# Attention rows exponentiated and scaled two groups ahead of their turns, and two copies of projected tiles moved ahead of squares and rows

## The chip, the cores and the metric

The kernel runs on one core of a Trainium2 chip. The metric is the device time of one execution in microseconds (us), the median of several executions; lower is better. The engines are TensorE (PE; its weight loads are listed as PEld), VectorE (DVE), ScalarE (ACT), GpSimd (POOL) and SyncE (SP), which only issues DMAs here.

## The reference

One inference step of a two-layer trunk over 1072 tokens: 1024 frames of a new stream, 16 meta tokens before it, and 32 frames of a running stream with 128 cached ones. Per layer, cut to what matters:

```python
h = rms_norm(x, gains[0])
z = h @ w_in          # q, k, v, indexer q/k/weights, conv B/C/x, gates
score = jnp.einsum('bqh,bqhl->bql', wi, jax.nn.relu(s))     # indexer
_, idx = lax.top_k(score, topk)                             # keys per query
p = jax.nn.softmax(jnp.where(valid, logits, -jnp.inf), axis=-1)
o = jnp.einsum('bqhgk,bqkhd->bqhgd', p, vg)                 # 8 heads over 2 key heads
m = jax.nn.sigmoid(ga) * y_a + jax.nn.sigmoid(gb) * y_b
x = x + rms_norm(m @ w_o, gains[1])
f = jnp.square(jax.nn.relu(rms_norm(x, gains[2]) @ w_up)) @ w_down
x = x + rms_norm(f, gains[3])
```

All of it is in float32; outputs are the new activations and the new keys, values, indexer keys and convolution states.

## The kernel before, in words

Activations are kept transposed: features on the 128 partitions, 8 feature tiles (`KT`), tokens along the free axis in three thirds of 358 columns (`side(i)`, `NCH`). Every matrix product is done in three passes of high and low parts: `H[:, 0]` is the rounded high part, made by ACT (`h_rows`, L1053), `H[:, 1]` the remainder, made by DVE (`lo` in `hn_rows`, L1561). Each engine runs a list of instructions written out by hand, in order; semaphores tie the lists together, so an instruction that waits holds back all that stand behind it on its engine.

**Projection.** `proj(n)` (L643, matmuls L660) multiplies token tile `ORDER[n]` (the 48 special tokens first, then tiles 0 to 7 of 128 tokens) by the 1092 columns of q, k, v and the indexer, into PSUM banks 0 to 2: 8 steps k of 9 matmuls. `proj(n + 1)` reuses the banks and so waits for `sb_copied`, which ACT's `copy_out(n)` (L1123) signals when it has copied the banks to `SB`. `put_v(n)` (L1137) then copies the values to `V`. `proj(1)` also waits until both parts of all eight H rows of the second third in time are there (`hq_hi`, `hq_lo`). While this runs, the norm of the last third is still being made: ACT squares the eight feature tiles (`edge_squares`, L1049), DVE adds them (in layer 0 L1532 and L1535), PE sums over partitions (`edge_sums`, L626) and broadcasts (L634), DVE scales (L1565), and ACT and DVE make the H rows of that third. DVE's `rotate` (L1638) applies the rotary embedding to `SB`, ACT's `stage` stores keys and values and makes `ST`, which PE transposes (L674); ACT copies the transposes to `IQ`, `IK` and `QH`. The indexer's scores (PE L692, ACT L1120, DVE L1684 and L1687) follow tile by tile.

**Search, convolution, gates.** DVE then finds the top-k thresholds by a bitwise search (L1836 and around), while PE does the convolution and gate products (L558) from weights that POOL splits (L440, L442).

**Attention.** The work is cut into 18 groups i = 2a + kv: query tile `ORDER[a]` (48 special tokens, then tiles 0 to 7) by key head kv, four query heads each. A group has as many *turns* as it has key tiles: 2 for a = 0 and 1, then 3, 4, ... 9. `STEPS` lists all turns in order. The stages of a row (group i, head g) are

- `logits(i, g)` on PE (L821), into one of two pairs of PSUM banks, so that a row waits for the masking of the row before last;
- `mask_row(i, g)` on DVE (L1900, and L1889 for the meta columns of the longest tile, g = -1): adds the mask, scales, and takes the least value;
- `exponent(i, g)` on ACT (L1284): exponential, with its sum;
- `normalise(i, g)` on DVE: reciprocal (L1909) and scaling (L1911).

A turn is `turn_p(u)` on PE (four transposes, L838), the copy to `PT` on ACT, and `values(u)` on PE (L850). After the last turn of a group DVE copies the result (`outputs`, L1921), ACT makes its high part (`o_hi_copy`) and DVE its remainder (`o_lo_part`, L1928).

The order on each engine before, for group i: PE does `logits(i + 2, g)` in turn min(g, n - 1), then the transposes of the next turn, then `values`. ACT, behind the PT copy of turn min(g, n - 1):

```python
copy(PT[0:w, u % 3, 0:GROUP * m], PS[0:w, 4 + u % 2, 0:GROUP * m]).then_inc(pt_made, 1)
for g in range(GROUP):
    if now + 1 < NGRP and min(g, n - 1) == kt:
        exponent(now + 1, g)
```

DVE, per group: `mask_row(i + 2, g)` and `normalise(i + 1, g)` in turn, with `outputs(i - 1)` behind the first mask row and `o_lo_part(i - 2)` behind the third. So a row is masked two groups ahead, and exponentiated and scaled one group ahead, and its last rows are scaled just before the group's first turn. The rows live in three sets of buffers (`prob`): groups i, i + 1 and i + 2 have one each.

## Time and profile before

| | |
|---|---|
| runs shown | 3441.95, 3443.53, 3445.90 us; median 3443.53 |
| profiled execution | 3440.69 us, its span 3438.9 us |
| busy over the span | PE 96%, PEld 91%, DVE 55%, ACT 22%, POOL 33% |
| chain that ended last | PE 88%, DVE 6%, ACT 2%, the rest 1 to 2% each |
| attention stages | about 557 to 751 us and 2256 to 2451 us |
| projection stages | begin of the span to about 220 us, and from about 1730 us |

The span is that of the profiled execution alone; its own time with what lies around it is in the table. In a timeline a row gives the start, the duration, the engine, the line, the operation with output and input, how often it follows itself, and in brackets how long the engine had been idle before it and what released it. In a table of windows the granted clock is a mean over the window between the two levels of TensorE, 1.00 being 2.4 GHz and 0.50 being 1.2 GHz.

### The profile page before, as it was taken

The page shows a single profiled execution, that of the slowest core. Times are in us where ns is not written, and L with a number is a line of the kernel's source. Part 1 is how long each engine was busy: PE and PEld are TensorE (multiplying, and loading weights), DVE is VectorE, ACT ScalarE, POOL GpSimd, SP SyncE. Part 2 cuts the span into 40 slices and gives each one's busy share as a digit, 9 for nine tenths or more (in the row PEclk, how much of TensorE's full clock was granted, in tenths as well). Part 3 has the DMA queues.
Part 4 walks back from the last instruction along what each step waited for, and adds up shares of the span by engine and source line. Part 5 has one row for each costly group of instructions (what it writes and reads, how often), then busy time and mean ns, then how long its engine had stood idle before and what let it go on. Part 6 is the DMA issues. An engine that isn't in the chain of part 4 may idle for free.

```text
span 3438.9 us, 48630 instructions
## 1 busy us (share of the span) xinstructions
PE 3288.3 (96%) x19268; PEld 3120.4 (91%) x19268; DVE 1883.4 (55%) x3093; ACT 770.1 (22%) x1370; POOL 1125.3 (33%) x517
## 2 busy tenths in 40 slices
PE   4999998999999999999969999989999999999997
PEld 4989997679999999999959999966799999999997
DVE  6259997644662332415562799966456614233245
ACT  4330113641320110101233201136314201011011
POOL 2023332005444333434420333310163434334460
PEclk8999998999999999999989999989999999999999
DMA  3121223013221111111331112220133111111113
GB/s 127 51 68 44 75 93 107 25 45 110 97 83 43 49 43 43 43 49 43 105 99 57 68 44 81 94 94 19 69 114 105 60 43 43 49 43 43 43 61 103
DMA packets 97867, 230.02 MB, mean 67 GB/s; under 512 B 13024, under 2 KB 54592, under 8 KB 97728
## 3 DMA queue, kind: packets, MB, share of 16 engines
q1 hardware_dynamic: 36448, 126.50, 11.3%
q10 hardware_dynamic: 61280, 101.61, 8.5%
q8 instruction: 94, 1.54, 0.2%
q14 instruction: 45, 0.37, 0.0%
HBM read 176.44 MB, written 51.65 MB: 66 GB/s over the span
## 4 chain that ended last, share of the span: by engine, by line
PE 88%; DVE 6%; ACT 2%; issue 2%; DMA 1%; POOL 1%; ACTq 1%; DVEq 0%; SPq 0%; POOLq 0%
PE PS L558 61%; PE PS L567 9%; PE PS L660 5%; PE PS L850 5%; PE PS L821 2%; PE PS L838 2%; PE PS L730 1%; PE PS L692 1%; PE PS L674 1%; DVE HN L1565 1%; DVE X L1610 1%; DVE H L1561 1%; DMA HN<-in_xT 1%; DVE X L1616 1%; ACT SB L1024 1%
## 5 line engine op out<-in xcount | busy, mean ns | idle before, releaser
L558 PE MATMUL PS<-H,W 128*128 128x358 f32 x8064 | 1329.8, 327 | 0.1
L558 PEld LDWEIGHTS PS<-H,W 128*128 128x128 f32 x8064 | 1327.6, 189 | 0.2
L440 POOL TENSOR_TENSOR W<-RAW,ones 128x1024 fp32r<-128x1024 f32 x184 | 358.7, 1949 | 1667.5 <-PE PS L558 1626.2
L558 PE MATMUL PS<-A,W 128*128 128x358 f32 x4608 | 760.1, 327 | 0.0
L558 PEld LDWEIGHTS PS<-A,W 128*128 128x128 f32 x4608 | 758.7, 189 | 1.5 <-issue 1.5
L442 POOL TENSOR_TENSOR W<-RAW,W 128x1024 fp32r<-128x1024 f32 x184 | 511.7, 2781 | 14.4
L1836 DVE TENSOR_SCALAR_CACHE_REDUCE PASS<-SC,TC,CST 128x400 bf16<-128x400 f32 x372 | 356.1, 1020 | 1.7
L660 PE MATMUL PS<-WQ,H 128*128 128x364 f32 (+1 forms) x1296 | 245.4, 346 | 46.2 <-ACT SB L1024 38.6
L660 PEld LDWEIGHTS PS<-WQ,H 128*128 128x128 f32 (+1 forms) x1296 | 219.1, 190 | 58.6 <-ACT SB L1024 41.5
L2000 DVE TENSOR_TENSOR SQ<-SQ,RS 128x1074 f32<-128x1074 f32 x64 | 117.8, 1841 | 263.6 <-ACT SQ L1410 257.8
L1410 ACT ACTIVATE SQ<-PS 128x1074 f32<-128x1074 f32 x64 | 68.4, 1069 | 808.9 <-PE PS L558 806.6
L2015 DVE TENSOR_TENSOR X<-X,PS 128x1074 f32 x32 | 40.8, 1274 | 306.6 <-PE PS L558 306.6
L2002 DVE TENSOR_TENSOR SQ<-SQ 128x1074 f32<-128x1074 f32 x64 | 205.8, 3216 | 2.2
L850 PE MATMUL PS<-PT,V 128*128 128x512 f32 (+3 forms) x368 | 202.5, 634 | 0.3
L567 PE MATMUL PS<-A,WD 128*128 128x358 f32 x1008 | 168.0, 327 | 0.0
L567 PE MATMUL PS<-H,WR 128*128 128x358 f32 x1008 | 168.0, 326 | 0.0
L567 PEld LDWEIGHTS PS<-A,WD 128*128 128x128 f32 x1008 | 165.1, 188 | 0.0
L567 PEld LDWEIGHTS PS<-H,WR 128*128 128x128 f32 x1008 | 164.5, 188 | 0.0
L821 PEld LDWEIGHTS PS<-KS,QS 128*128 128x128 f32 (+1 forms) x480 | 87.3, 206 | 79.2 <-issue 60.7
L821 PE MATMUL PS<-KS,QS 128*128 128x512 f32 (+6 forms) x480 | 145.0, 425 | 6.1 <-DMA QS<-qs_keep 3.4
L1024 ACT ACTIVATE A<-SQ 128x1074 f32 (+1 forms) x64 | 70.6, 1103 | 341.7 <-DVE SQ L2002 341.7
L1024 ACT ACTIVATE PT<-PS 128x512 f32<-128x512 f32 (+3 forms) x184 | 107.4, 584 | 159.4 <-PE PS L838 159.2
(182 smaller groups left out, 2938.3 us busy)
## 6 DMA issues: line engine op xcount, KB each, us to landing
RAW<-in_w_slab SPq DMA_DIRECT2D x216, 512.0 KB, 3.5
gates<-GS ACTq DMA_DIRECT2D x32, 537.0 KB, 3.0
x_keep<-X ACTq DMA_DIRECT2D x9, 1432.0 KB, 7.3
GA<-gates ACTq DMA_DIRECT2D x16, 537.0 KB, 3.6
GB<-gates ACTq DMA_DIRECT2D x16, 537.0 KB, 4.5
ALO<-x_keep ACTq DMA_DIRECT2D x6, 1432.0 KB, 7.3
qs_keep<-QH ACTq DMA_DIRECT2D x16, 512.0 KB, 2.6
QS<-qs_keep ACTq DMA_DIRECT2D x16, 512.0 KB, 3.6
```

The lines of the kernel that those rows point to most:

```text
L440: g_.tensor_tensor(hi, raw, one, ALU.mult).then_inc(hi_split, 1)
L442: g_.tensor_tensor(lo, raw, hi.bitcast(F32), ALU.subtract).then_inc(raw_split, 1)
L558: mm = nc.tensor.matmul(PS[:, b0 + c, 0:CW], W[:, s, w, k, :], act[:, a, k, c * CW:(c + 1) * CW], start=(first and w == 0 and a == 0), sto ...
L567: mm = nc.tensor.matmul(PS[:, bank_, 0:CW], w[:, h, k, :], act[:, a, k, c * CW:(c + 1) * CW], start=(k == first and h == 0 and a == 0), st ...
L660: last = nc.tensor.matmul(PS[0:m, b, 0:QG], H[:, a, k, t * P:t * P + m], WQ[:, k, w, b * QG:(b + 1) * QG], start=(k == 0 and w == 0 and a ...
L821: last = nc.tensor.matmul(flat[0:m, c0 + dst:c0 + dst + w], QS[:, a % 3, GROUP * kv + q, 0:m], KS[:, 2 * kv + x, key:key + w], start=(x == ...
L838: last = nc.tensor.transpose(PS[0:w, 4 + u % 2, g * m:(g + 1) * m], prob(PA, i, g)[0:m, dst:dst + w], cst["ident"][0:m, 0:m])
L850: nc.tensor.matmul(PS[:, 6 + kv, 0:GROUP * m], V[0:w, vt, :], PT[0:w, u % 3, 0:GROUP * m], start=(kt == 0), stop=(kt == len(key_tiles(t)) ...
L1024: return nc.scalar.activation(out, in_, ACT.Copy)
L1836: did(V_.tensor_scalar(PASS[0:m, SC_OFF[t]:SC_OFF[t] + EXT[t]], row(t), at_least, cst["negk"][0:m, c:c + 1], op, ALU.add, accum_out=CNT[0: ...
L2000: V_.tensor_tensor(SQ[:, s, :], SQ[:, s, :], RS[:, :], ALU.mult).then_inc(up_scaled, 1)
L2002: V_.tensor_tensor(SQ[:, s, :], SQ[:, s, :], SQ[:, s, :], ALU.mult).then_inc(up_sq, 1)
```

## The change

1. *Attention.* `rows_at(u)` lists the rows whose logits PE does in turn u; PE's own order is what it was. ACT now does the exponentials of those rows behind the PT copy of turn u + 1, and DVE scales them in turn u + 1, both for group i + 2. DVE's start order mixes the mask rows of group 1 with the scaling of group 0, and `outputs` and `o_lo_part` are placed by turn.
2. *Projection.* In layer 0 the copy of tile 0 and of its values stand after six of the eight H rows of the second third, ahead of the last two, of `past_split` and of the squares of the last third; in layer 1 they stand after two of those squares. In both layers the copy of tile 1 stands after four of the last third's H rows. No instruction is added or taken away.

```diff
--- before.py
+++ after.py
@@ -378,6 +378,13 @@
         STEPS = [(a, kv, kt) for a in range(9) for kv in range(NKV) for kt in range(len(key_tiles(ORDER[a])))]
         NU = len(STEPS)
 
+        def rows_at(u):
+
+            a, kv, kt = STEPS[u]
+            n = len(key_tiles(ORDER[a]))
+            return [(j, g) for j, g in ROW_UNITS if j == NKV * a + kv + 2 and min(max(g, 0), n - 1) == kt]
+
+
         ENDS = [u + 1 for u, (_, _, kt) in enumerate(STEPS) if u + 1 == NU or STEPS[u + 1][2] == 0]
 
         def raw_q(l, k):
@@ -856,11 +863,9 @@
                     if i < 2:
                         logits(i, g)
                 turn_p(0)
-                for u, (a, kv, kt) in enumerate(STEPS):
-                    i, n = NKV * a + kv, len(key_tiles(ORDER[a]))
-                    for j, g in ROW_UNITS:
-                        if j == i + 2 and min(max(g, 0), n - 1) == kt:
-                            logits(j, g)
+                for u in range(NU):
+                    for j, g in rows_at(u):
+                        logits(j, g)
                     if u + 1 < NU:
                         turn_p(u + 1)
                     values(u)
@@ -1100,9 +1105,7 @@
             wq_high(0, range(5, 6))
             edge_root(0, 0, 1)
             wq_high(0, range(6, 8))
-            h_rows(0, 1, range(KT))
-            past_split(0)
-            edge_squares(0, 2, range(KT))
+            h_rows(0, 1, range(6))
 
             for l in range(DEPTH):
 
@@ -1165,26 +1168,36 @@
                     wq_high(l, range(6, 7))
                     h_rows(l, 1, range(4, KT))
                     wq_high(l, range(7, 8))
-                    edge_squares(l, 2, range(KT))
+                    edge_squares(l, 2, range(2))
+                    copy_out(0)
+                    put_v(0)
+                    edge_squares(l, 2, range(2, KT))
                 def cc_copy(j):
                     act.wait_ge(slab_done, l * NDONE + S_CONV + 3 * j + 1)
                     if j:
                         act.wait_ge(conv_drained, l * 8 + 2 * j - 1)
                     copy(ch(CC[:, :]), bank(conv_bank(3 * j))).then_inc(cc_drained, 1)
 
-                copy_out(0)
+                if l == 0:
+                    copy_out(0)
+                    put_v(0)
+                    h_rows(0, 1, range(6, KT))
+                    past_split(0)
+                    edge_squares(0, 2, range(KT))
                 act.wait_ge(past_lo, (l + 1) * 2)
                 act.dma_start(d["ks_keep"][:, :, PAST0:NKEY], KH[:, :, :].bitcast(F32)).then_inc(past_stored, 16)
-                put_v(0)
                 edge_root(l, 0, 2)
                 stage(0)
-                h_rows(l, 2, range(KT))
+                h_rows(l, 2, range(4))
+                copy_out(1)
+                h_rows(l, 2, range(4, KT))
                 act.wait_ge(hq_lo, (l + 1) * NCH * KT)
                 if l:
                     act.wait_ge(edge_stored, l * NCH * 16)
                 for n, t in enumerate(ORDER):
                     m, nn = ROWS[t], l * 9 + n
-                    copy_out(n + 1)
+                    if n:
+                        copy_out(n + 1)
 
                     act.wait_ge(turned, l * 27 + 3 * n + 1)
                     if n:
@@ -1286,19 +1299,20 @@
 
                 for g in range(GROUP):
                     exponent(0, g)
+                behind = [(1, g) for g in range(GROUP)]
                 i = 0
                 for u, (a, kv, kt) in enumerate(STEPS):
-                    t, now = ORDER[a], NKV * a + kv
-                    m, w, n = ROWS[t], key_tiles(t)[kt][2], len(key_tiles(t))
+                    t = ORDER[a]
+                    m, w = ROWS[t], key_tiles(t)[kt][2]
                     if kv == 0 and kt == 0 and 0 < a < 7:
                         q_load(a + 2)
                     act.wait_ge(turned_p, l * NU + u + 1)
                     if u >= 3:
                         act.wait_ge(pv_done, l * NU + u - 2)
                     copy(PT[0:w, u % 3, 0:GROUP * m], PS[0:w, 4 + u % 2, 0:GROUP * m]).then_inc(pt_made, 1)
-                    for g in range(GROUP):
-                        if now + 1 < NGRP and min(g, n - 1) == kt:
-                            exponent(now + 1, g)
+                    for j, g in behind:
+                        exponent(j, g)
+                    behind = [(j, g) for j, g in rows_at(u) if g >= 0]
                     if i + 1 < len(ENDS) and u == ENDS[i + 1] + 1:
                         o_hi_copy(i)
                         i += 1
@@ -1929,24 +1943,29 @@
                                      A[:, 0, 2 * kv:2 * kv + 2, t * P:t * P + m].bitcast(F32),
                                      ALU.subtract).then_inc(o_lo, 1)
 
-                for i, g in ROW_UNITS:
-                    if i < 2:
-                        mask_row(i, g)
                 for g in range(GROUP):
+                    mask_row(0, g)
+                for g in range(GROUP):
+                    mask_row(1, g)
                     normalise(0, g)
                 dve.wait_ge(gates_stored[0], (l + 1) * 8 * 16 + 16)
                 dve.wait_ge(gates_stored[1], (l + 1) * 8 * 16 + 16)
                 V_.memset(A[:, :, 0:4, NTOK:T].bitcast(F32), 0.0).then_inc(pads_zero, 1)
-                for i in range(NGRP + 1):
-                    for g in range(-1, GROUP):
-                        if (i + 2, g) in ROW_NO:
-                            mask_row(i + 2, g)
-                        if g == 0 and i:
+                behind = [(1, g) for g in range(GROUP)]
+                for u, (a, kv, kt) in enumerate(STEPS):
+                    i, n, rows = NKV * a + kv, len(key_tiles(ORDER[a])), rows_at(u)
+                    for x in range(max(len(rows), len(behind), 1)):
+                        if x < len(rows):
+                            mask_row(*rows[x])
+                        if x == 0 and kt == 0 and i:
                             outputs(i - 1)
-                        if g == 2 and i > 1:
-                            o_lo_part(i - 2)
-                        if g >= 0 and i + 1 < NGRP:
-                            normalise(i + 1, g)
+                        if x < len(behind):
+                            normalise(*behind[x])
+                    behind = [(j, g) for j, g in rows if g >= 0]
+                    if kt == min(2, n - 1) and i > 1:
+                        o_lo_part(i - 2)
+                outputs(9 * NKV - 1)
+                o_lo_part(9 * NKV - 2)
                 o_lo_part(9 * NKV - 1)
```

**ACT, layer 0, around the copy of tile 0** (`SB<-PS`; H rows are those of the second third, `SQE` the squares of the last). Before:

```order
L1024 ACTIVATE H_70<-HN_71 128x358 x8
L1024 ACTIVATE IK<-PR 128x128
L1024 ACTIVATE KH<-PR 128x2x128
L1049 ACTIVATE SQE<-X 128x358 x8
L1024 ACTIVATE SB<-PS 48x1092
L1177 DMA ks_keep<-KH 512x1x128
L1024 ACTIVATE V<-SB 48x128
L1030 ACTIVATE MEANC<-PS 120x3
```

Now:

```order
L1029 ACTIVATE H_70<-HN_71 128x358 x6
L1029 ACTIVATE SB<-PS 48x1092
L1029 ACTIVATE V<-SB 48x128
L1029 ACTIVATE H_70<-HN_71 128x358 x2
L1029 ACTIVATE IK<-PR 128x128
L1029 ACTIVATE KH<-PR 128x2x128
L1054 ACTIVATE SQE<-X 128x358 x8
L1188 DMA ks_keep<-KH 512x1x128
L1035 ACTIVATE MEANC<-PS 120x3
```

The copy to SB and the one to V moved ahead of two H rows, the two past copies and the eight squares.

**ACT, layer 0, around the copy of tile 1** (`SB<-PS 128x1092`). Before:

```order
L1024 ACTIVATE ST<-SB 48x12x64
L1024 ACTIVATE ST<-SB 48x3x64 x2
L1024 ACTIVATE H_70<-HN_71 128x358 x8
L1024 ACTIVATE SB<-PS 128x1092
L1024 ACTIVATE IQ<-PS 128x4x48
L1024 ACTIVATE IK<-PS 128x2x16
L1024 ACTIVATE IK<-PS 128x2x48
```

Now:

```order
L1029 ACTIVATE ST<-SB 48x12x64
L1029 ACTIVATE ST<-SB 48x3x64 x2
L1029 ACTIVATE H_70<-HN_71 128x358 x4
L1029 ACTIVATE SB<-PS 128x1092
L1029 ACTIVATE H_70<-HN_71 128x358 x4
L1029 ACTIVATE IQ<-PS 128x4x48
L1029 ACTIVATE IK<-PS 128x2x16
L1029 ACTIVATE IK<-PS 128x2x48
```

The copy moved ahead of four H rows of the last third; `IQ` and `IK` stand right behind those rows.

**ACT and DVE in attention, group 4** (three turns; rows of 272 columns belong to group 5, those of 400 columns to group 6; `PA_74` and `PB` hold the rows, `O_75` the result). ACT before:

```order
L1024 ACTIVATE PT<-PS 128x512
L1284 ACTIVATE PB,DEN<-PB,LEAST 128x272
L1024 ACTIVATE PT<-PS 128x512
L1284 ACTIVATE PB,DEN<-PB,LEAST 128x272
L1024 ACTIVATE A_59<-O_75 128x2x128
L1024 ACTIVATE PT<-PS 16x512
L1284 ACTIVATE PB,DEN<-PB,LEAST 128x272 x2
L1024 ACTIVATE PT<-PS 128x512
```

ACT now:

```order
L1029 ACTIVATE PT<-PS 128x512
L1297 ACTIVATE PB,DEN<-PB,LEAST 128x272 x3
L1029 ACTIVATE PT<-PS 128x512
L1297 ACTIVATE PA_74,DEN<-PA_74,LEAST 128x400
L1029 ACTIVATE A_59<-O_75 128x2x128
L1029 ACTIVATE PT<-PS 16x512
L1297 ACTIVATE PA_74,DEN<-PA_74,LEAST 128x400
L1029 ACTIVATE PT<-PS 128x512
L1297 ACTIVATE PA_74,DEN<-PA_74,LEAST 128x400 x2
L1029 ACTIVATE PT<-PS 128x512
```

DVE before, the first turns of group 4:

```order
L1900 ISA PA_74,LEAST<-PS,MB 128x400
L1900 ISA LEAST 128x1
L1921 COPY O_75<-PS 64x256 x2
L1909 RECIPROCAL RDEN<-DEN 128x1
L1911 TENSOR_SCALAR PB<-PB,RDEN 128x272
L1900 ISA PA_74,LEAST<-PS,MB 128x400
L1900 ISA LEAST 128x1
L1909 RECIPROCAL RDEN<-DEN 128x1
L1911 TENSOR_SCALAR PB<-PB,RDEN 128x272
L1900 ISA PA_74,LEAST<-PS,MB 128x400
L1900 ISA LEAST 128x1
L1928 TENSOR_TENSOR A_59<-O_75,A_59 128x2x128
```

DVE now:

```order
L1914 ISA PA_74,LEAST<-PS,MB 128x400
L1914 ISA LEAST 128x1
L1935 COPY O_75<-PS 64x256 x2
L1923 RECIPROCAL RDEN<-DEN 128x1
L1925 TENSOR_SCALAR PB<-PB,RDEN 128x272
L1923 RECIPROCAL RDEN<-DEN 128x1
L1925 TENSOR_SCALAR PB<-PB,RDEN 128x272
L1923 RECIPROCAL RDEN<-DEN 128x1
L1925 TENSOR_SCALAR PB<-PB,RDEN 128x272
L1914 ISA PA_74,LEAST<-PS,MB 128x400
L1914 ISA LEAST 128x1
L1923 RECIPROCAL RDEN<-DEN 128x1
```

On ACT, group 5's last exponentials stand in group 4's first turn, and those of group 6 in the two behind it and in group 5's first. On DVE, three scalings of group 5 stand between the first and the second mask row of group 6, and each scaling of group 6 stands one turn behind its mask row.

## Rows read from the trace of the kernel before

**Rows 1.** Timeline, first layer, tile 0: start, length, engine, line, operation [idle before]

```profile
50.96 1.68 PE L660 MATMUL PS<-WQ,H 128*48 128x364 f32 x9 [1.14 <-POOL WQ L447]
...
55.38 1.40 DVE L1561 TENSOR_TENSOR H<-HN,H 128x358 fp32r<-128x358 f32 x3
55.49 0.50 ACT L1024 ACTIVATE H<-HN 128x358 fp32r<-128x358 f32 x1 [0.44 <-DVE HN L1565]
...
56.41 4.65 ACT L1049 ACTIVATE SQE<-X 128x358 f32<-128x358 f32 x8
...
60.96 1.06 ACT L1024 ACTIVATE SB<-PS 48x1092 f32<-48x1092 f32 x1
...
62.07 9.02 PE L660 MATMUL PS<-WQ,H 128*128 128x364 f32 x36 [9.44 <-ACT SB L1024]
```

**Rows 2.** Timeline, first layer, the copy of tile 1

```profile
83.09 1.08 ACT L1024 ACTIVATE SB<-PS 128x1092 f32<-128x1092 f32 x1 [0.82 <-DVE H L1561]
...
84.22 5.28 PE L660 MATMUL PS<-WQ,H 128*128 128x364 f32 x18 [5.03 <-ACT SB L1024]
84.28 0.35 ACT L1024 ACTIVATE IK<-PS 128x32 fp32r<-128x32 f32 x2
...
89.43 1.07 PE L674 MATMUL PS<-identr,ST 48*128 48x48 f32 x8
```

**Rows 3.** Timeline, second layer, the copies of tiles 0 and 1

```profile
1750.26 2.32 PE L660 MATMUL PS<-WQ,H 128*48 128x364 f32 x9 [4.29 <-POOL WQ L447]
...
1759.70 0.50 ACT L1049 ACTIVATE SQE<-X 128x358 f32<-128x358 f32 x1 [0.88 <-DVE X L1549]
...
1760.32 1.07 ACT L1024 ACTIVATE SB<-PS 48x1092 f32<-48x1092 f32 x1
...
1761.42 0.31 ACT L1024 ACTIVATE V<-SB 48x128 f32<-48x128 f32 x1
...
1761.44 7.68 PE L660 MATMUL PS<-WQ,H 128*128 128x364 f32 x36 [8.86 <-ACT SB L1024]
...
1782.25 4.56 PE L660 MATMUL PS<-WQ,H 128*128 128x364 f32 x18 [5.03 <-ACT SB L1024]
```

**Rows 4.** Windows of attention: length, busy PE, PEld, DVE, ACT, POOL; granted clock

```profile
584.60:595.30 10.70, 9.53 (x29) 5.29 (x28) 4.98 (x21) 4.21 (x13) 0.00 (x0) 0.68 0.09 35
595.30:603.00 7.70, 6.17 (x28) 3.66 (x27) 5.19 (x20) 4.14 (x12) 0.00 (x0) 1.00 0.06 10
603.00:624.60 21.60, 18.92 (x81) 12.37 (x80) 13.30 (x43) 10.86 (x27) 0.00 (x0) 0.84 0.07 23
624.60:637.10 12.50, 11.41 (x49) 7.30 (x48) 8.02 (x24) 6.33 (x16) 0.00 (x0) 0.86 0.12 41
637.10:646.70 9.60, 9.60 (x47) 6.21 (x46) 6.93 (x20) 6.57 (x14) 0.00 (x0) 1.00 0.00 0
725.30:738.20 12.90, 12.74 (x55) 6.84 (x54) 4.90 (x11) 9.80 (x18) 0.00 (x0) 1.00 0.00 0
2295.30:2337.10 41.80, 36.49 (x154) 23.36 (x153) 26.47 (x85) 21.47 (x54) 0.00 (x0) 0.88 0.09 26
```

**Rows 5.** Waits of PE in the first layer's attention: total us, times, longest

```profile
PE PS L838 <- DVE PA L1911: 6.7, 11, 1.1
PE PS L838 <- DVE PB L1911: 2.8, 4, 1.1
```

**Rows 6.** Timeline, DVE's first mask row of the first layer

```profile
557.66 0.33 DVE L1900 CUSTOM_DVE_ANT_0 PA<-PS,MB 48x176 f32<-48x176 f32 x1 [5.29 <-PE PS L821]
```

**Rows 7.** Timeline, first layer, the last mask row of group 15

```profile
719.00 1.16 ACT L1284 ACTIVATE PA<-PA,LEAST 128x1040 f32<-128x1040 f32 x1
...
721.09 1.28 DVE L1900 CUSTOM_DVE_ANT_0 PB<-PS,MB,TAIL 128x1024 f32<-128x1024 f32 x1
...
722.03 0.60 ACT L1024 ACTIVATE PT<-PS 128x512 f32<-128x512 f32 x1 [0.70 <-PE PS L838]
...
723.13 0.59 PE L850 MATMUL PS<-PT,V 128*128 128x512 f32 x1
```

## The prediction

> **What bounds the kernel now.** The page comes first: TensorE (PE) is busy for 96% of the span and the chain that ended last runs through it for 88%, so only time in which PE waits, or runs at its lower clock, can be won. Two kinds of place hold such time.
>
> The timeline of the first layer's projection shows the first. Tile 0's projection ends on PE at 52.6 us; the next matmul starts at 62.07, released by the copy to SB [rows 1]. ACT does that copy at 60.96, since eight H rows (the last at 55.49) and eight squares (from 56.41, 4.65 us) stand before it in ACT's order [rows 1]. A second hole follows: PE waits 5.03 us until 84.22 for the copy of tile 1, which ACT starts at 83.09 after all H rows of the last third [rows 2]. The second layer has both again: 8.86 us until 1761.44 and 5.03 us until 1782.25 [rows 3].
>
> The windows of the attention stage show the second place. I number its (tile, key head) groups 0 to 17. Group 9 runs its five turns in 9.60 us with PE busy throughout and the clock at 1.00; group 8, with the same five turns, takes 12.50 us at 0.86, group 4 takes 10.70 at 0.68, and group 5, of the same three turns, 7.70 at 1.00 [rows 4]. The waits name the cause: the first turn of a group waits for the scaling (L1911) of its own rows, 15 times and 9.5 us in the first layer [rows 5]. The second layer repeats this: 41.8 us from 2295.3 with PE busy 36.49, against 36.50 in the same 41.8 us of the first [rows 4].
>
> **Projection, first layer.** Six H rows now stand before the copy. Row 6 of the eight ends near 54.1 (the last begins at 55.49, and they follow each other about every 0.95 us), so the SB copy runs 54.1 to 55.2 (1.06 us [rows 1]) and V's copy (0.31 [rows 3]) to 55.5. PE's next projection also needs the two H rows left behind, 0.5 us each, and the two remainders that DVE takes from them, under 0.5 us each [rows 1]: 56.5, then 57.0. PE starts at 57.0 instead of 62.07: **5.0 us**. The squares start some 0.8 us late and end near 61.9 with DVE's sums behind them; PE wants the sum after 36 matmuls, not before 63, so they cost nothing; if that cover went, the 0.8 us would show.
>
> Tile 1's copy moves before H rows 4 to 7. ACT waits 0.44 us between such rows for DVE anyway, so four rows later it is where it was, and the IQ and IK copies come 1 us earlier: IK was done at 84.63, now near 83.7. PE's 18 matmuls start near 79.7 and are through by then, and the turns behind IK start near 83.8 instead of 89.43 [rows 2]: **5.6 us**. What is late next there is IK's copy.
>
> **Projection, second layer.** The copy stands behind two squares only and starts when the projection ends, near 1752.7 (1750.26 plus 2.32). PE resumes at 1753.9 instead of 1761.44: **7.5 us** [rows 3]. The six later squares begin 1.3 us late; ACT has 0.88 us of waiting at each [rows 3] and catches up after two. The sum that PE needs is ready near 1761, as PE arrives after 36 matmuls. The second hole closes as in the first layer, where IK would be done 0.5 us before PE's old restart (83.7 against 84.22 [rows 2]): here 1781.8, so that the turns start near 1781.9 instead of 1782.25 plus the 4.56 us of the 18 matmuls [rows 3]: **4.9 us**. DMA issues that ACT passes (ks_keep, x_keep, the store of tile 0's rows) keep their order; the x_keep store is issued at most 0.2 us later. Together 5.0 + 5.6 + 7.5 + 4.9 = **23.0 us**. DVE's search and POOL's splits follow PE and move with it.
>
> **Attention.** Exponentials and scaling are done one group earlier, so the 9.5 us of waits for L1911 go [rows 5]. PE's idle time in groups 4 to 8 is 1.17 + 1.53 + 2.68 + 1.09 = 6.5 us; the rest of the excess is the lower clock [rows 4]. Bounds: with neither, group 8 takes group 9's 9.6 us, groups 6 and 7 (four turns each) 7.7 us, and groups 4 and 5 PE's busy 6.2 us of group 5: 15.4 + 9.6 + 12.4 = 37.4 instead of 52.5 us, 15.1 less. If DVE, whose order and work in the small groups stay tight (5.19 us busy of group 5's 7.70 [rows 4]), takes the waits over, nothing. I take 3 of 6.1 us in groups 4 and 5, because DVE's 5.19 us would fill most of 6.2 and PE will still pause, and 7 of 9.0 in groups 6 to 8, because there DVE is busy only 13.30 of 21.60 and 8.02 of 12.50 us: **10 us**. What PE did before the clock was low in groups 4 and 6 to 8 was to pause for such waits, while group 9 had none and stayed at 1.00. The Trainium skill, "TensorE: Matmul & The Clock Gate", HAM oscillation, prices throttled time at half of itself: the shares below 1.00 in these windows make 17.3 us at the lower level, which by that page would give back 8.6 us, with the 6.5 us idle 15.1 us instead of my 10.
>
> Against it stand two new waits. At the start DVE scales group 0's rows between the mask rows of group 1 instead of behind them; four mask rows of 0.33 us and their reads [rows 6] come into the chain to the first turn: **-1.4 us**. Groups 1 to 3 I leave at nothing: they are short chains of DVE and ACT before and after; up to 2 us either way.
>
> In the long groups an exponential now waits on ACT for a mask row of the same turn, and the next PT copies queue behind it. In group 15 the last mask row ends on DVE at 722.4 (the new order brings it to about 722.1); an exponential of 1.16 us then ends near 723.5, while the PT copy behind it ran at 722.03 and PE's matmul with it at 723.13 [rows 7]. PE is held until 724.2: 1.1 us, also in group 14; with masks a tenth shorter 0.3 in groups 12 and 13: **-2.8 us**. Group 16, which did exponentials of group 17 on turns without logits, took 12.9 us [rows 4]; nine turns at the pace of turns with neither, 1.30 us (ACT's PT copy of 0.60 and its 0.70 of waiting before it [rows 7]), take 11.7: **+1.2 us**. Sum per layer 10 - 1.4 - 2.8 + 1.2 = 7.0, both layers **14 us**.
>
> **The sum.** 23 + 14 = 37 us off the profiled execution's 3440.69, which lies 2.8 us under the median of the three runs, 3443.53; from the median 3406.5.
>
> **The rivals.**
> *The clock stays up.* If the new order leaves no pauses, groups 4 to 8 give all 15.1 us and each layer 12.1: 23 + 24 = 47 us, 3396; without the late stalls 3391. For it: group 9, without a wait, ran at 1.00. Against: DVE has as much to do as before in groups 1 to 5. The page named above stands on this side.
> *The waits only change their name.* DVE's order in the small groups holds masks back behind three scalings in a row, PE waits for a mask instead of a scaling, and the clock falls as before: attention gives nothing, 3420.5.
> *The search caps the first part.* DVE had waited 5.29 us when attention began [rows 6]. If its search did not move with the projection, a layer could give no more than that: 10.6 instead of 23 us, 3419. Against: the search starts when the last scores are added, behind PE's projection.
> *The copy isn't what PE waits for.* If another row held tile 1's projection, only the second holes would close: 10.5 + 14, 3419. The releaser named is the copy in all four.
> *Slower.* ACT's wait for masks holds PE at every row of the long groups. Eight groups (8 to 15) have four rows, 32 a layer, with masks of 0.7 to 1.28 us: at 1.0 us each 64 us, against gains of 23 + 2 x 9.8 = 42.6: 3465. It decides from 0.67 us of PE per row. Against: in a turn with logits PE does these between ACT's PT copy and the matmul that needs it, a cover that only the last row of a group lacks.
>
> **How the numbers follow.** Forecast 0.60 (3398 to 3416); clock stays up 0.17; only names change 0.12; search or another wait 0.07; slower 0.03; exactly cancelling 0.01. The range takes in the first four cases but for their edges: 3388 to 3422. A change under 0.2% (7 us, about what a measurement here can tell) needs nearly all of 37 us to vanish: faster 0.95, same 0.02, slower 0.03.
>
> **What would show it.** Right: PE's waits for the SB copies near 4.4, 0.6, 1.3 and 0.6 us; no wait for the scaling after group 1; groups 6 to 8 under 28 us; group 16 near 11.7 us; new waits of PE for PT copies in groups 12 to 15. Wrong: waits of PE for masks over 5 us a layer, a clock under 0.9 in groups 6 to 8, or ACT idle for masks in every row of the long groups with PE idle behind it.

## The result and the profile after

| | before | after |
|---|---|---|
| median of the paired runs, us | 3442.74 (4 runs) | 3386.03 (4 runs, 3384.59 to 3387.57) |
| profiled execution, us | 3440.69 | 3384.59 |
| its span, us | 3438.9 | 3382.8 |
| mean granted clock over the span | 0.976 | 0.985 |

The ratio is 0.9837, with an interval of 0.982 to 0.9854: 56.7 us faster where 37 were forecast, 2 us under the low end of the range. The direction was right and the size was not.

The page of the changed kernel says that the same engine bounds it:

```profile
PE 3261.9 (96%) x19268; PEld 3105.5 (92%) x19268; DVE 1886.0 (56%) x3093; ACT 772.9 (23%) x1370; POOL 1125.0 (33%) x517
...
PE 88%; DVE 5%; ACT 2%; issue 2%; DMA 2%; POOL 1%; ACTq 1%; SPq 0%; DVEq 0%; POOLq 0%
```

**Projection.** PE's timeline in the first layer, and below it the second, answers to [rows 1 to 3] (start, length, engine, line, operation, and in brackets the idle time before it and what ended it):

```profile
56.89 8.38 PE L667 MATMUL PS<-WQ,H 128*128 128x364 f32 x36 [4.34 <-DVE H L1575]
...
73.76 3.25 PE L667 MATMUL PS<-WQ,H 128*128 128x364 f32 x18 [0.40 <-ACT SB L1029]
77.88 1.07 PE L681 MATMUL PS<-identr,ST 48*128 48x48 f32 x8 [0.87 <-ACT IK L1029]
...
1725.26 2.94 PE L667 MATMUL PS<-WQ,H 128*48 128x364 f32 x9 [4.01 <-POOL WQ L454]
1729.36 8.42 PE L667 MATMUL PS<-WQ,H 128*128 128x364 f32 x36 [1.16 <-ACT SB L1029]
...
1746.27 3.25 PE L667 MATMUL PS<-WQ,H 128*128 128x364 f32 x18 [0.40 <-ACT SB L1029]
1750.39 1.07 PE L681 MATMUL PS<-identr,ST 48*128 48x48 f32 x8 [0.87 <-ACT IK L1029]
```

The reader sees the holes of 9.44, 8.86, 5.03 and 5.03 us shrink to 4.34, 1.16, 0.40 and 0.40, and a new wait for the copy to IK, as forecast.

**Attention.** The windows of the changed kernel: groups 1 to 3, 4 to 8, 9 to 11, 12 to 15 and 16 of the first layer, then 1 to 3 and 4 to 8 of the second (start and end, length, busy time of PE, PEld, DVE, ACT, POOL, granted clock):

```profile
555.72:571.52 15.80, 13.74 (x61) 10.12 (x61) 10.63 (x54) 8.56 (x32) 0.00 (x0) 0.76 0.27 86
571.52:609.28 37.76, 37.76 (x180) 24.43 (x179) 31.56 (x105) 27.98 (x69) 0.00 (x0) 0.95 0.09 29
609.28:640.85 31.57, 31.57 (x152) 20.51 (x151) 23.60 (x60) 22.72 (x46) 0.00 (x0) 1.00 0.06 17
640.85:698.61 57.76, 57.13 (x261) 36.27 (x260) 38.11 (x93) 37.29 (x67) 0.00 (x0) 1.00 0.03 10
698.61:710.63 12.02, 12.02 (x56) 6.77 (x54) 1.28 (x3) 5.67 (x10) 0.00 (x0) 1.00 0.00 0
...
2228.42:2244.22 15.80, 13.66 (x62) 10.05 (x61) 10.63 (x54) 8.56 (x32) 0.00 (x0) 0.76 0.27 78
2244.22:2281.97 37.75, 37.75 (x180) 24.50 (x179) 31.56 (x105) 27.97 (x69) 0.00 (x0) 0.95 0.09 29
```

The same groups of the kernel before, 4 to 8 of both layers and then 1 to 3 of both (the rows in [rows 4] were cut at rounder times):

```profile
584.58:637.08 52.50, 46.03 (x180) 28.62 (x179) 31.49 (x105) 25.56 (x65) 0.00 (x0) 0.84 0.08 28
2286.44:2337.10 50.66, 44.61 (x180) 28.01 (x180) 31.23 (x104) 25.45 (x64) 0.00 (x0) 0.86 0.07 22
566.74:584.58 17.84, 15.46 (x61) 10.28 (x61) 10.31 (x54) 8.43 (x32) 0.00 (x0) 0.72 0.21 67
2265.63:2286.44 20.81, 18.82 (x61) 11.84 (x61) 10.67 (x54) 8.56 (x32) 0.00 (x0) 0.58 0.21 71
```

In groups 4 to 8 PE now never stands still. PE's busy time itself fell too, from 46.03 to 37.76 us for the same 180 matmuls, and most of that is the clock. Not all: group 5 ran at 1.00 in both kernels and was busy 6.17 us before and 5.82 now. What is left of the low clock (0.95) lies in group 4, between 573.5 and 577.5 us; PE's last wait for a mask, 1.41 us, ended at 571.16. What PE still waits for in the first layer's attention, in answer to [rows 5]:

```profile
PE PS L828 <- DVE LEAST L1914: 4.0, 4, 1.5
PE PS L828 <- DMA QS<-qs_keep: 1.7, 1, 1.7
PE PS L845 <- DVE PA L1925: 0.7, 2, 0.4
PE PS L857 <- ACT PT L1029: 0.6, 2, 0.3
```

Of the 9.5 us for the scaling 0.7 are left, in group 0. Mask rows (L1914) hold PE for 4.0 us, all of it before group 4. The wait for the PT copy is the new one of the long groups, and it is small.

**Where the 56.1 us of the two spans lie**, in order of time:

| stretch | gained, us |
|---|---|
| to the first attention's first logits (557.14, now 545.29) | 11.85 |
| first attention (192.3, now 176.5) | 15.8 |
| from there to the last step of tile 0's projection (1750.26, now 1725.26) | -2.6 |
| from there to the turns behind IK (1786.74, now 1750.39) | 11.4 |
| to the second attention (2256.06, now 2218.17) | 1.5 |
| second attention (193.4, now 176.3) | 17.1 |
| the rest | 1.1 |

### The profile page after: what moved, and what is told of

The parts are those of the page before. It is cut to its first block, busy times and chain, and to the rows that moved or that the text cites. A ratio compares the mean times of both kernels' runs of the same rounds, so it can differ in the third digit from the quotient of the medians.

```text
span 3382.8 us, 48630 instructions
## 1 busy us (share of the span) xinstructions
PE 3261.9 (96%) x19268; PEld 3105.5 (92%) x19268; DVE 1886.0 (56%) x3093; ACT 772.9 (23%) x1370; POOL 1125.0 (33%) x517
## 4 chain that ended last, share of the span: by engine, by line
PE 88%; DVE 5%; ACT 2%; issue 2%; DMA 2%; POOL 1%; ACTq 1%; SPq 0%; DVEq 0%; POOLq 0%
PE PS L565 62%; PE PS L574 8%; PE PS L667 5%; PE PS L857 5%; PE PS L828 3%; PE PS L845 2%; PE PS L737 1%; PE PS L699 1%; DVE X L1624 1%; DVE X L1630 1%; PE PS L681 1%; DVE HN L1579 1%; DMA HN<-in_xT 1%; DMA HN<-x_keep 1%; DVE H L1575 1%
## 5 line engine op out<-in xcount | busy, mean ns | idle before, releaser
L667 PEld LDWEIGHTS PS<-WQ,H 128*128 128x128 f32 (+1 forms) x1296 | 216.1, 188 | 36.8 <-ACT SB L1029 14.7
L857 PE MATMUL PS<-PT,V 128*128 128x512 f32 (+3 forms) x368 | 193.5, 609 | 1.3 <-ACT PT L1029 1.3
L2024 DVE TENSOR_TENSOR A<-SQ,A 128x1074 f32 x64 | 83.3, 1302 | 97.9 <-ACT A L1029 97.9
```

The costliest lines, as they stand in the source:

```text
L667: last = nc.tensor.matmul(PS[0:m, b, 0:QG], H[:, a, k, t * P:t * P + m], WQ[:, k, w, b * QG:(b + 1) * QG], start=(k == 0 and w == 0 and a ...
L857: nc.tensor.matmul(PS[:, 6 + kv, 0:GROUP * m], V[0:w, vt, :], PT[0:w, u % 3, 0:GROUP * m], start=(kt == 0), stop=(kt == len(key_tiles(t)) ...
L2024: V_.tensor_tensor(A[:, 1, jj, :].rearrange("p a n -> p (a n)"), SQ[:, s, :], A[:, 0, jj, :].bitcast(F32).rearrange("p a n -> p (a n)"), A ...
```

## The experiments

The theory under test (the "clock stays up" rival of the prediction, made sharper): the low clock in groups 4 to 8 follows PE's pauses of about 1 us at the first turns, so to take a pause away returns it and the slow matmuls behind it. Its rival: a pause costs only itself, and the rest comes from the other part of the change or from the new order. Group n in what follows is the window from group n's first transposes to those of the next.

**The two parts apart.** Two kernels: the one before with only the second part of the change (projection), and with only the first (attention).

> The kernel before with the projection part of the change alone (copies of tiles 0 and 1 moved), attention as before. The first attention should start near 545.3 as in the changed kernel (11.9 us earlier), the second layer's projection give another 12 to 13. Theory A (the parts are independent): 24 us off the kernel before, 3416 to 3419, attention stages unchanged at 192 to 193 us. Rival B (an earlier start of the stages also changes what attention meets, for instance DMA loads of keys and queries that now come late, so that part of the 33 us of attention or the missing 2.6 us between the layers belongs here): attention stages differ from 192.3 and 193.4 by more than 1 us, or the total is under 21 or over 27 us.

> The kernel before with the attention part alone (exponentials and scaling two groups ahead), projection as before. Theory A: attention 176.4 us a layer instead of 192.3 and 193.4, so 32 to 33 us off: 3408 to 3411; groups 4 to 8 take 37.8 us with the clock at 0.95. My prediction's terms would give 14 us, 3429. If the 2.6 us that were lost between the first layer's attention and the second's projection come with this part, they show here as a shift that shrinks between 750 and 1750 us.

Measured against the kernel before (3442.3 us, nine runs): the projection part 3420.15 us (five runs), ratio 0.9933 (0.9919 to 0.9946); the attention part 3407.71 (four runs), ratio 0.99 (0.9885 to 0.9915). That is 22.2 and 34.6 us, together 56.7: the parts add up. The projection part is what I had priced (23.0); the attention part is two and a half times what I had (14). The medians match theory A to about 1 us. In the first kernel's profile the sign of rival B shows all the same: its first attention took 194.4 us instead of 192.3. It has the same attention code and 9.0 us of waits for the scaling (9.5 before); the 2 us lie in groups 1 to 3, which took 19.80 us at a clock of 0.62 instead of 17.84 at 0.72. Its second attention is as before (193.4). Its five runs lie between 3411.2 and 3421.5.

The second attention of the second kernel shows what groups 4 to 8 take when the clock does not fall in them:

```profile
2267.73:2304.53 36.80, 36.38 (x181) 23.48 (x179) 31.47 (x105) 28.04 (x69) 0.00 (x0) 1.00 0.09 30
```

**Tile 0's copy alone.**

```diff
 (the projection part, but in both layers)
-                h_rows(l, 2, range(4))
-                copy_out(1)
-                h_rows(l, 2, range(4, KT))
+                h_rows(l, 2, range(KT))
```

> The kernel before with only the copy of tile 0 moved (tile 1's behind all H rows of the last third, as before). By my terms this gives 5.0 us in the first layer and 7.5 in the second, the second holes staying: the first attention starts near 552 instead of 557.1, the whole 12 to 13 us less, span 3426. Rival (without tile 1's copy the first hole's gain is only moved to the second, since PE waits there for H rows that follow the squares): under 5 us in all, span over 3433.

3432.32 us in a single run beside 3440.48, so 8.2 us: between the two expectations. The holes closed as priced, PE's restart lying at 57.00 in the first layer and 4.1 us behind the last step in the second (11.18 before). The rest was given back: 1.1 us in the first attention (193.4), 1.9 before the second projection, most of it by the clock (its place is shown at the end of the next section), and some 2 us between the second restart and the second attention.

**Which engine made the pause.** ACT as changed, DVE's loop as before.

```diff
 (the changed kernel, DVE's order of the kernel before)
-                    for x in range(max(len(rows), len(behind), 1)):
-                        if x < len(rows):
-                            mask_row(*rows[x])
-                        ...
+                for i in range(NGRP + 1):
+                    for g in range(-1, GROUP):
+                        if (i + 2, g) in ROW_NO:
+                            mask_row(i + 2, g)
+                        ...
+                        if g >= 0 and i + 1 < NGRP:
+                            normalise(i + 1, g)
```

> The changed kernel with ACT's exponentials two groups ahead but DVE's order of the kernel before: the scaling stays one group ahead, each behind the mask row of the same head. Theory A (the pause at a group's first turn is DVE's: the last scalings stand behind the last mask rows, which wait for PE's last logits of the group): the waits for the scaling come back, 7 to 9.5 us a layer, with the clock at 0.84 to 0.88 in groups 4 to 8 (about 51 us), and late groups 14 and 15 keep their 15.9 us; the span is 24 to 30 us above the changed kernel's 3382.8. Rival B (the exponentials on ACT were what the scaling waited for): the waits nearly vanish, groups 4 to 8 take under 41 us and the span stays within 8 us of 3382.8.

The waits of PE in its first attention, and its groups 4 to 8:

```profile
PE PS L845 <- DVE PA L1925: 6.8, 12, 1.1
PE PS L845 <- DVE PB L1925: 2.8, 4, 1.1
PE PS L857 <- ACT PT L1029: 2.1, 4, 0.8
```

```profile
572.85:625.15 52.30, 45.83 (x181) 28.72 (x180) 31.49 (x105) 27.47 (x69) 0.00 (x0) 0.84 0.09 27
```

The full 9.6 us of waits are back and the clock is at 0.84. The exponentials alone bring nothing (3419.0 us of span, 3418.4 with the projection part alone); the pause was DVE's, whose last scalings of a group stood behind the mask rows of PE's last logits. The span is 36 us over the changed kernel, more than the 24 to 30 expected: groups 1 to 3 lost 1.3 and 5.0 us and the late groups 2 us a layer (14 and 15 take 16.6 us each).

**The pause filled, nothing made earlier.** This is the run that parts the theories.

```diff
 (the kernel before, in turn_p)
                         if kt == 0:
+                            for _ in range(6 if 4 <= i <= 8 and g >= 2 else 0):
+                                nc.tensor.matmul(PS[:, 4 + u % 2, g * P:(g + 1) * P], identr[:], identr[:],
+                                                 start=True, stop=True)
                             pe.wait_ge(p_ready, (l * NGRP + i) * GROUP + g + 1)
```

> The kernel before with six extra 128x128 matmuls on the identity (their result is overwritten) ahead of the waits for the scaling of the third and fourth row of the first turn of groups 4 to 8; nothing is made ready any earlier, PE is only kept busy through its pauses. Clock theory (the pauses are what the low clock follows): the granted clock of groups 4 to 8 rises from 0.84 to over 0.93 and they take 3 to 8 us less than 52.5 us a layer, although PE does more; the waits that are left are those of DVE, 4 to 6 us. Rival (the low clock has to do with what PE runs there, such as short rows and transposes, or comes at fixed times): clock stays 0.84 and groups 4 to 8 take 52 to 56 us.

Groups 4 to 8 of both layers:

```profile
587.90:635.50 47.60, 46.88 (x240) 32.94 (x240) 31.16 (x104) 25.42 (x64) 0.00 (x0) 0.92 0.08 23
2279.77:2325.79 46.02, 45.25 (x240) 31.76 (x239) 31.33 (x105) 25.56 (x65) 0.00 (x0) 0.96 0.10 31
```

PE does 60 matmuls more in each layer and is through 4.9 and 4.6 us earlier; the clock rose from 0.84 and 0.86 to 0.92 and 0.96. The single run took 3428.78 us, about 13 under the kernel before.

Group by group the evidence is uneven. Clean are groups 7 and 8: 1.6 us less each, in both layers, at 1.00 instead of 0.84 and 0.86. The first row is the kernel before, the second the filled one, both in the first layer:

```profile
614.25:637.08 22.83, 20.72 (x88) 13.43 (x87) 14.13 (x42) 11.72 (x28) 0.00 (x0) 0.85 0.08 24
```

```profile
615.88:635.50 19.62, 19.62 (x113) 13.97 (x112) 13.98 (x43) 11.73 (x28) 0.00 (x0) 1.00 0.09 28
```

No input was ready earlier, so this gain is the clock's. Group 6 took 11.28 us at 0.85 in both layers, as before; a wait of 0.35 us had stayed in it. In the first layer group 4 gained 3.3 us, but group 5 lost 1.65 (9.36 us at 0.82) and groups 1 to 3, which have no fill, took 20.75 us instead of 17.84, so that this attention as a whole gained only 1.8 us. In the second layer groups 1 to 3 happened to be short (17.18 us instead of 20.81), and the whole gained 8.2. So the fill moves some of the low stretches and removes others.

**The pause put back.**

```diff
 (the changed kernel, in turn_p)
+                    if kt == 0 and 4 <= i <= 8:
+                        pe.wait_ge(masked, (l * NGRP + i + 1) * GROUP + GROUP)
                     for g in range(GROUP):
```

> The changed kernel with a pause put back: in groups 4 to 8 PE waits before the first turn's transposes until DVE has masked the row whose logits PE has just issued, about 1 us each. Clock theory: the granted clock of groups 4 to 8 falls from 0.95 towards the 0.84 to 0.86 of before and they take 45 to 50 us instead of 37.8 in each layer, clearly more than the waits themselves (4 to 6 us). Rival (a pause costs only itself): 42 to 44 us, clock still 0.93 or more.

Groups 4 to 8, and PE's wait in those of the first layer (named "issue", since the wait is at an instruction of its own):

```profile
571.90:618.55 46.65, 41.78 (x178) 25.98 (x179) 30.79 (x100) 27.76 (x69) 0.00 (x0) 0.89 0.08 24
2253.73:2301.77 48.04, 43.47 (x179) 27.68 (x179) 31.05 (x100) 27.70 (x69) 0.00 (x0) 0.86 0.08 23
```

```profile
PE PS L847 <- issue: 5.6, 5, 1.5
```

These windows are 8.9 and 10.3 us longer than in the changed kernel, and the clock fell to 0.89 and 0.86. The first of the five pauses ends where the window begins, so it is not in them: from the first logits to the last `values` the two attentions are 9.8 and 11.2 us longer, for 5.6 and 5.3 us of waiting, and the span grew by 20.7 us. On average a pause costs 1.7 to 2.1 times itself here. But not each: in the first layer groups 5 to 7 had pauses of 1.38, 1.47 and 1.16 us and kept the clock, and took 4.0 us more for 4.0 us of waiting:

```profile
582.45:607.36 24.91, 21.43 (x106) 13.66 (x107) 17.88 (x59) 16.41 (x40) 0.00 (x0) 1.00 0.10 26
```

The clock was low in groups 4 and 8 of that layer, and in groups 4, 6, 7 and 8 of the second. So pauses of this size bring the clock down, often and not always; the rival that a pause costs only itself holds where it stays up.

**The same pause in longer groups.** A first edit waited, in groups 9 to 13, for masks that were long done, and made no pause.

> The pause of the earlier experiment in groups 9 to 13 instead of 4 to 8, where groups are longer and the clock was 1.00: about 1 to 1.5 us of waiting in each. If a pause every 10 to 13 us also lets the clock fall, groups 9 to 13 (57.4 us) take 68 us or more, with the clock at 0.93 or lower; if the low clock needs the short groups of 4 to 8, they take 63 to 65 us with the clock at 0.98 or more.

Groups 9 to 11 stayed at 31.57 us: no information on the question. The second edit waits for the mask row just issued:

```diff
+                    if kt == 1 and 9 <= i <= 13:
+                        pe.wait_ge(masked, (l * NGRP + i + 2) * GROUP + 1)
```

> The earlier late pause waited for masks that were long done. Here the pause is real: in groups 9 to 13 of the changed kernel PE waits, before the second turn's transposes, for the mask row whose logits it has just issued, about 1.0 to 1.3 us each, 5 to 6 us a layer. If a pause every 10 to 13 us also lets the clock fall, groups 9 to 13 (57.4 us together) take 68 us or more, clock 0.93 or lower; if the low clock needs pauses as close together as in groups 4 to 8, they take 62 to 64 us with the clock at 0.98 or more.

Groups 9 to 13 took 67.6 and 65.8 us (57.4 without pauses) with 6.0 us of waiting in each layer. Groups 10 and 12 of the second layer, and group 10 of the first:

```profile
2304.48:2316.86 12.38, 11.21 (x54) 7.16 (x53) 8.61 (x22) 8.27 (x17) 0.00 (x0) 1.00 0.14 44
...
2329.24:2345.18 15.94, 14.64 (x60) 9.02 (x59) 9.26 (x20) 8.98 (x17) 0.00 (x0) 0.89 0.12 33
...
622.13:636.15 14.02, 12.85 (x53) 8.12 (x52) 8.61 (x22) 8.22 (x17) 0.00 (x0) 0.88 0.13 37
```

The same group 10 with the same pause takes 12.38 us in one layer and 14.02 in the other: 1.64 us is what one fall of the clock costs here. It fell in groups 10 and 11 of the first layer and in group 12 of the second, three times behind ten pauses. So neither expectation holds as it stands: the short groups are not needed, and not every pause of 1 us lets the clock fall.

**The start of attention.** The changed kernel still has low clock in its first 20 us and 3.8 to 4.0 us of waits for masks there. Two tries.

```diff
 (the changed kernel, fills; those in group 0's first transposes and before three later rows left out)
...
+                for _ in range(12):
+                    nc.tensor.matmul(PS[:, 5, 0:P], identr[:], identr[:], start=True, stop=True)
                 for i, g in ROW_UNITS:
                     if i < 2:
+                        for _ in range(3 * (i + g > 0)):
+                            nc.tensor.matmul(PS[:, 5, 0:P], identr[:], identr[:], start=True, stop=True)
                         logits(i, g)
...
```

> The changed kernel with matmuls on the identity (results overwritten) in PE's remaining pauses at the start of attention: 12 while it waits for the queries, 3 before each of seven logits rows and before three first transposes of group 0, 4 before the fourth row of three later groups. Clock theory: the clock of 0.50 to 0.76 in the first 25 us of attention rises towards 1.00 and groups 1 to 3 take 12 to 14 us instead of 15.8, each layer 3 to 8 us less. Rival (short rows of 48 queries hold the clock down whatever PE does between, or the fills cost what they bring): each layer the same within 1 us, or up to 3 us longer.

3386.97 us, ratio 0.9842 (0.9826 to 0.9858): nothing gained. The first attention took 3.6 us more than in the changed kernel, the second 0.6 less. A window of its first attention:

```profile
548.00:564.00 16.00, 16.00 (x73) 13.30 (x71) 8.81 (x52) 7.28 (x31) 0.10 (x1) 0.50 0.53 193
```

PE was busy for all of these 16 us, the first half of them with fills, and the clock stayed at its lower level, 1.2 GHz. In the second attention the clock was at 1.00 through the start, where the changed kernel has it low, and fell near 2226 us, while PE was busy. So filled pauses held it up for some microseconds in one layer and not in the other, and in neither through the groups of 48 queries; on the sum the rival holds. Why is open; a fill with wider matmuls was not tried.

```diff
 (the changed kernel: ACT from group 10 on, and DVE, whose start order is that of the kernel before)
-                    behind = [(j, g) for j, g in rows_at(u) if g >= 0]
+                    behind, held = held, [(j, g) for j, g in rows_at(u) if g >= 0]
+                    if NKV * a + kv < 10:
+                        behind, held = behind + held, []
...
+                        if (i + 2, g) in ROW_NO:
+                            mask_row(i + 2, g)
+                        ...
+                        while g >= 0 and scaled < min(GROUP * (i + 1) + g + 2, GROUP * NGRP):
+                            normalise(*divmod(scaled, GROUP))
+                            scaled += 1
```

> The changed kernel with (a) DVE scaling one row behind every mask row, three rows late, its start order as before the change, and (b) ACT in groups 10 and later doing a row's exponential two turns after its logits instead of one. Theory: the start takes 4.4 instead of 5.0 to 5.2 us, PE's 2.3 to 2.5 us a layer of waits for masks after the start shrink below 1 us, and groups 14 and 15 go back from 15.95 to 15.4 us, 12 and 13 from 12.93 to 12.8, as then no PT copy stands behind an exponential that waits for a mask: 3 to 5 us a layer less, 3376 to 3381. Rival (the late groups grew because of DVE's order, not ACT's): 14 and 15 stay at 15.9 us.

3386.69 us, ratio 0.9841 (0.9824 to 0.9857): no gain in the sum, but each term can be read. The start fell to 4.5 and 4.4 us, groups 12 and 13 to 12.77 and 12.79 (as before the change), 14 and 15 to 15.7. Against that the later scaling brought the pauses back:

```profile
570.90:611.51 40.61, 38.34 (x180) 24.63 (x179) 31.46 (x105) 27.80 (x69) 0.00 (x0) 0.96 0.11 35
```

```profile
PE PS L845 <- DVE PA L1927: 2.8, 4, 0.9
...
PE PS L845 <- DVE PB L1927: 0.8, 1, 0.8
```

Groups 4 to 8 take 2.8 us more than in the changed kernel, with PE idle for 2.3 us of them. Groups 5 and 6 kept 1.00 with their pauses: here too a pause cost about itself. That groups 14 and 15 kept 0.3 us each over the kernel before although PE waits for nothing there is not explained.

**A version of the good parts,** beside the changed kernel on the same chip: DVE's old start, the later exponentials and scaling from group 10 on only, and a fill of twelve matmuls in PE's 2 us pause in the merge.

> The changed kernel once more, on the chip of the next two: 3384 to 3388, attention 176 to 177 us a layer. Whether the clock falls behind the pauses in the merge of the first layer (about 388 us after the first attention's start) is open: it did in five of six profiled programs, not in that of the kernel before.

> The changed kernel with what the experiments suggest: DVE's start order of the kernel before; from group 10 on exponentials two turns after their logits and the scaling one row behind every mask row; and twelve matmuls on the identity in PE's 2 us pause for the mean of the merge's second third. Theory: the start takes 4.4 to 4.6 us (0.6 less a layer), groups 12 to 15 give 0.8 us a layer back, groups 4 to 8 stay at 37.8 us, and in the merge the clock stays up (2.2 us in the layers where it fell): 3 to 6 us under the changed kernel, 3379 to 3383. Rival (another start shifts the stretches of low clock, and the fill changes nothing): the same within 2 us.

The changed kernel again 3386.63 us (0.984, 0.9826 to 0.9854), this version 3381.16 (0.9826, 0.9812 to 0.984), its five runs from 3379.95 to 3382.62 against 3382.29 to 3387.34: 5.5 us between the medians, and the fastest of the study, though the intervals of the ratios overlap. Attention took 175.0 and 174.8 us (176.4 and 176.0), which is 2.6 us of it; where the other 2.9 lie the two profiles, 1.6 us of span apart, don't show. The fill in the merge did not do what it was for: the pause shrank from 1.99 to 0.64 us, and the clock fell all the same.

## Why the prediction was wrong

| step | forecast, us | measured |
|---|---|---|
| projection, first layer | 5.0 + 5.6 | 5.2 + 6.4 |
| projection, second layer | 7.5 + 4.9 | 7.1 + 4.3 |
| groups 4 to 8, per layer | 10 (at most 15.1) | 14.7 and 12.9 |
| groups 1 to 3 | 0 (up to 2 either way) | 2.0 and 5.0 |
| start of attention | -1.4 | -0.8 and -0.65 |
| groups 12 to 15 | -2.8 | -1.45 |
| group 16 | 1.2 | 0.95 |
| groups 9 to 11 | 0 | 0.3 |

**Right.** The projection, with PE idle for 4.34, 0.40, 1.16 and 0.40 us at the four restarts, where 4.4, 0.6, 1.3 and 0.6 were named. That the sum is 23.0 us for 23.0 forecast is luck in part: the first layer gave 1.0 us more and the second 1.0 less. The scaling's waits ended after group 0. Groups 6 to 8 take 24.55 us, under 28; group 16 takes 12.0. The rival of masks that take the waits' place came true only before group 4 (4.0 us, under the 5 named as the limit). The rival on the slower side is refuted by the waits for PT copies, 0.6 us a layer and not 32.

**Wrong: the term "3 of 6.1 us in groups 4 and 5, and 7 of 9.0 in groups 6 to 8".** The windows of [rows 4] leave 6.0 and 9.1 us rather than 6.1 and 9.0. Measured are 5.2 and 9.6 us in the first layer, 3.3 and 9.6 in the second, where group 4 had been shorter (8.81 us). The term had mixed two doubts into one discount. DVE's 5.03 us of busy time in group 4's 7.39 us did not hold PE at all, as the window's PE busy time equals its length; the same is so in group 5, with 5.15 of 5.82. And the clock's part was taken at a fraction though the profile of before pointed to the pauses (with group 5, which paused for 1.5 us and ran at 1.00, against it). The runs settle that: pauses filled, groups 7 and 8 are 3.2 us shorter in each layer; pauses put back, 9.8 and 11.2 us are lost for 5.6 and 5.3 of waiting. The bound was the value to take: 14.7 of 15.1 us in the first layer, and in the second, where groups 4 to 8 had been 50.66 us long, 12.9 of 13.3. It was not a floor: with the clock at 1.00 throughout, these groups took 36.80 us and not 37.4.

The Trainium skill, "TensorE: Matmul & The Clock Gate", HAM oscillation, prices throttled time at half of itself, and the estimate made with it, 8.6 us and the 6.5 us idle, lies 0.4 us over the 14.7 measured. The trace agrees with it only nearly, since 3.8 us at the lower level are left (0.95 of 37.76 us): for what went, the same estimate gives 13.2 us. The Trainium skill, on the same page, "A second HAM failure mode", describes short idle times of PE between groups of matmuls that make the clock swing. The filled and the restored pauses bear this out in most places, and groups 5 to 7 of the restored ones, at 1.00, do not.

**Wrong: "Groups 1 to 3 I leave at nothing".** They are short chains, but 17.84 us at 0.72 and 20.81 at 0.58 held the same two losses as groups 4 to 8. In the second layer PE's idle time there hardly changed (2.0, now 2.1 us); its busy time fell from 18.82 to 13.66. So these 5.0 us are mostly clock (group 1 is 0.8 us shorter at 0.50 in both kernels; in group 3 the clock went from 0.63 to 1.00), and I had not looked at the clock of these windows. The size is luck in part: these groups took 17.1 to 20.9 us in the old order of DVE, from one attention to the next, and 15.8 to 16.4 in that of the change.

**Wrong in size: the two new waits.** An exponential does wait for its mask and hold the PT copy, as this stretch of ACT and PE in group 15 shows, in answer to [rows 7]:

```profile
694.56 1.16 ACT L1297 ACTIVATE PB<-PB,LEAST 128x1040 f32<-128x1040 f32 x1 [0.49 <-DVE LEAST L1914]
...
695.72 1.07 ACT L1029 ACTIVATE PT<-PS 128x512 f32<-128x512 f32 x2
...
696.35 1.13 PE L857 MATMUL PS<-PT,V 128*128 128x512 f32 x2 [0.32 <-ACT PT L1029]
```

But PE still had a matmul of the turn before and four transposes to do meanwhile, so 0.58 us a group reach it instead of 1.1. The start cost 0.8 and 0.65 us where 1.4 were named.

The terms add up: 18.9 of the 19 us missed are in attention (32.9 against 14). Of these, 7.6 are the discount in groups 4 to 8, 7.0 groups 1 to 3, 4.0 the two new waits that came out smaller, and the rest lies in groups 9 to 11 and 16. Groups 1 to 3, which no rival had priced, are also why the result lies under the 3391 of the rival with all of the 15.1 us and no late stalls. The 2.6 us lost between the layers are mostly one more swing of the clock. At the end of the merge's first norms PE makes nearly the same pauses in both kernels; the first two rows are the kernel before, the last two the changed one:

```profile
973.17 0.73 PE L567 MATMUL PS<-H,W 128*128 128x358 f32 x3 [1.28 <-DVE H L1605]
974.87 5.40 PE L567 MATMUL PS<-H,W 128*128 128x358 f32 x30 [0.97 <-ACT H L1369]
```

```profile
945.56 1.08 PE L574 MATMUL PS<-H,W 128*128 128x358 f32 x3 [1.28 <-DVE H L1619]
947.25 7.56 PE L574 MATMUL PS<-H,W 128*128 128x358 f32 x30 [0.61 <-ACT H L1383]
```

The same thirty matmuls take 5.40 or 7.56 us. The slow form also stands in the profiles of the changed kernel run again, of tile 0's copy alone and of the last version, so the profile of the kernel before had been lucky in that place. Another 0.9 us lie at the start of the second layer, between PE's sum at 1728.80 and its broadcast at 1740.58 (11.78 us apart, now 12.70), 0.7 of them in eighteen matmuls that took 4.94 us and now 5.67; some 0.5 came back elsewhere.

## What to carry to other kernels

Where a profile shows PE pauses of about a microsecond and a granted clock under 1.00 in the same windows, price the pause and the slow matmuls behind it together: the time to reach is the busy time at full clock, and a discount belongs only to pauses that another engine will put back. Such a price is an average: single pauses of 1.2 to 1.5 us cost only themselves here. Read the clock of every window next to the one in question, the dull ones too. And ask of each wait which engine's order makes it: here the exponentials, moved alone, gained nothing, because the scaling's place on DVE set the pause.

## What was unexpected of the hardware

- A pause of 1 us is enough for the clock to fall, but not always: the same group with the same pause took 12.38 us or 14.02. Swings of this kind, in places with the same code and waits, move whole stages by 2 to 3 us (groups 1 to 3 in the old order: 17.2, 17.8, 19.8 or 20.8 us in different attentions). They are probably a good part of the spread of some 8 us among runs of one kernel: of seven runs of the kernel before, the fastest, 3436.43 us, had a mean granted clock of 0.978 and the slowest, 3444.88, of 0.974. Which stages differ in them is not shown, as only one run of each was profiled.
- A busy PE does not by itself get the higher clock back: 16 us of unbroken matmuls, those of the groups of 48 queries with 128x128 fills between the first of them, ran at 0.50 at the start of attention, while in groups 4 to 8 low stretches ended after a few microseconds.
